# Expert weights loaded in pairs of pieces, the last expert's down product by column halves, and six unread products around the router

## The reference

```
def moe_swiglu(x, w_router, w_gate, w_up, w_down):
    logits = (x @ w_router).astype(jnp.float32)
    top_val, top_idx = lax.top_k(logits, TOP_K_EXPERTS)
    gate = jax.nn.softmax(top_val, axis=-1)
    ...
    for e in range(N_EXPERTS):
        out = out + combine[..., e:e + 1] * swiglu(x, w_gate[e], w_up[e], w_down[e])
    return out
...
    y = rms_norm(x, p['norm_final'])      # x * rsqrt(mean(x*x) + 1e-6) * gain
```

## Time and profile before

| | |
|---|---|
| median of 3 runs | 1419.91 us (1419.84 to 1422.66) |
| the profiled execution | 1420.81 us |
| its span, first to last instruction | 1419.0 us |
| PE busy | 1365.2 us, 96% of the span |
| DVE, ACT, POOL busy | 613.5, 235.9, 224.2 us |
| chain that ended last | PE 89%, DVE 8%, issue 1%, ACT 1% |
| the experts' stretch | from 718.66 us (first L1782) to 1403.4 us |
| expert weights | 384 loads of 704 KB, median 15.0 to 18.6 us from issue to landing |

### The profile page before, as it was taken

How to read it: one execution, slowest core, us unless ns; L and a number is a source line. 1 busy time by engine, 2 the same in 40 slices (tenths; PEclk the granted TensorE clock), 3 DMA queues, 4 the chain that set the end, 5 groups by cost and what they waited for, 6 DMA issues and landing times.

```text
span 1419.0 us, 39988 instructions
## 1 busy us (share of the span) xinstructions
PE 1365.2 (96%) x18034; PEld 981.8 (69%) x18034; DVE 613.5 (43%) x1252; ACT 235.9 (17%) x547; POOL 224.2 (16%) x271
## 2 busy tenths in 40 slices
PE   7899999999999999888899999999999999999996
PEld 5667899999997778777545656566565665656553
DVE  3599378677648467736232212120131202212153
ACT  3144121211016212413200000101000010000102
POOL 5147002121001433152030000000000000000100
PEclk9999999999999999989999999999999999999999
DMA  9554053433453300108969999999999999999992
GB/s 377 182 190 119 1 223 136 178 123 117 164 178 106 119 17 3 62 22 317 357 238 391 403 414 403 414 414 402 414 401 414 403 413 415 392 411 406 410 395 102
DMA packets 86020, 377.66 MB, mean 266 GB/s; under 512 B 11967, under 2 KB 12959, under 8 KB 85594
## 3 DMA queue, kind: packets, MB, share of 16 engines
q1 hardware_dynamic: 77712, 353.77, 63.8%
q0 software_dynamic: 4832, 17.17, 3.3%
q10 hardware_dynamic: 3306, 4.17, 0.8%
HBM read 367.15 MB, written 7.91 MB: 264 GB/s over the span
## 4 chain that ended last, share of the span: by engine, by line
PE 89%; DVE 8%; issue 1%; ACT 1%; DMA 0%; SPq 0%; DVEq 0%
PE bk L1782 32%; PE bk L1799 16%; PE bk L824 10%; PE bk L1081 10%; PE bk L1697 2%; PE bk L1029 2%; PE bk L1366 1%; DVE left L2409 1%; DVE tops L2407 1%; PE bk L1287 1%; PE bk L1248 1%; PE bk L1240 1%; PE bk L1232 1%; PE bk L1222 1%; PE bk L1214 1%
## 5 line engine op out<-in xcount | busy, mean ns | idle before, releaser
L1782 PE MATMUL bk<-part,xe 128*32 128x352 f32 x6144 | 458.9, 459 | 2.4 <-DVE xe L2972 2.4
L1782 PEld LDWEIGHTS bk<-part,xe 128*32 128x32 f32 x6144 | 252.7, 110 | 203.8 <-issue 105.5
L1799 PE MATMUL bk<-part,hidT 128*32 128x256 f32 x4224 | 232.6, 379 | 0.0
L1799 PEld LDWEIGHTS bk<-part,hidT 128*32 128x32 f32 x4224 | 151.6, 109 | 78.4 <-issue 1.0
L3040 DVE TENSOR_TENSOR hp<-sg,bk 128x352 f32<-128x352 f32 x48 | 37.3, 776 | 352.9 <-PE bk L1782 352.9
L824 PE MATMUL bk<-mx,ring 128*128 128x288 f32 x384 | 98.3, 415 | 0.0
L824 PE MATMUL bk<-xg,ring 128*128 128x288 f32 x336 | 87.5, 420 | 8.9 <-DMA ring<-in_weights 8.5
L824 PEld LDWEIGHTS bk<-mx,ring 128*128 128x128 f32 x384 | 73.4, 194 | 21.2 <-issue 0.8
L3066 DVE COPY ye<-bk 32x256 f32<-32x256 f32 x48 | 20.3, 422 | 150.8 <-PE bk L1799 150.1
L824 PEld LDWEIGHTS bk<-xg,ring 128*128 128x128 f32 x336 | 64.8, 196 | 27.8 <-issue 9.2
L3311 POOL TENSOR_TENSOR free_rows<-row_ss 128x1 f32 x7 | 5.4, 768 | 471.1 <-DVE xe L2981 447.1
(11 more groups left out here) (598 smaller groups left out, 1647.3 us busy)
## 6 DMA issues: line engine op xcount, KB each, us to landing
part<-in_moe_gate SPq DMA_DIRECT2D x128, 704.0 KB, 18.6
part<-in_moe_up SPq DMA_DIRECT2D x128, 704.0 KB, 18.0
part<-in_moe_down SPq DMA_DIRECT2D x128, 704.0 KB, 15.0
ring<-in_weights SPq DMA_DIRECT2D x121, 512.0 KB, 5.8
ro<-in_weights SPq DMA_DIRECT2D x8, 512.0 KB, 8.6
expert_rows<-ye ACTq DMA_DIRECT2D x7, 384.0 KB, 7.0
Ss<-in_states SPq DMA_DIRECT2D x1, 2048.0 KB, 7.9
out_wkv_sample<-Ss SPq DMA_DIRECT2D x8, 256.0 KB, 2.5
```

What stands on the lines that cost most here:

```text
L1782: last = mm(banks[g][32 * c:32 * c + 32, 0:FQ], xe[:, k, 32 * g:32 * g + 32], parts[PART_OF[ph]][:, FH * k + FQ * c:FH * k + FQ * c + FQ], ...
L1799: last = mm(down_bk[g // 2][32 * q:32 * q + 32, 256 * (g % 2):256 * (g % 2) + 256], hidT[:, half, g, 32 * m:32 * m + 32], parts[PART_OF[ph ...
```

## The change

Four things change.

1. **Layout and loads.** The gate, up and down weights of all experts are laid out ahead of the launch as one array `experts` [8 experts, 6 phases, 4 pairs, 128 partitions, 2816 numbers]. SP loads a pair of pieces with one transfer of 128 rows of 11264 bytes (`pair_load`), 192 transfers in place of 384, once PE has used both pieces of the pair 24 back.
2. **The last expert's down product** runs in column halves (`narrow_columns`): of each quarter of 256 columns, first the lower 128 of all 22 row blocks (into the down banks), then the upper 128 (into the gate banks). Between the last two passes PE scatters the lower half. `scatter`, `add_rows` and the end of the kernel take the columns as these interleaved halves; the squares of the lower half are summed, and `acc` times gain is formed (`acc_g`), while PE still works on the upper half.
3. **The end of the kernel** is by halves as well: ACT does the lower half (`first_columns`), DVE the upper one, the epsilon goes in with the root's bias, and the transfers wait for both. DVE's adding of the returned rows of experts 0 to 5 moves behind `hidden(0)` and `rows_turned` of the last expert.
4. **Six unread products** on PE: two behind L1717, two behind L1728 (512 and 256 columns), two behind the gather.

```
+def expert_pairs(inputs):
+    gate, up, down = (np.asarray(inputs[f"moe_{n}"])[0] for n in ("gate", "up", "down"))
+    wide = lambda w: w.reshape(NE, KC // 2, 2, P, 2, FH).transpose(4, 0, 1, 3, 2, 5)
+    low = down.reshape(NE, 2, P, KC // 2, 2 * FH).transpose(1, 0, 3, 2, 4)
+    packed = np.zeros((NE, 6, KC // 2, P, 2 * FH), np.float32)
...
-    SCATTER = ((0, 0), (0, 1), (1, 0), (1, 1), (2, 0), (2, 1))
+    SCATTER = ((0, 0), (1, 0), (2, 0), (0, 1), (1, 1), (2, 1))
-    DONE_AT = (2, 4, 6)
+    DONE_AT = (4, 5, 6)
+    columns = lambda x, half: x.rearrange("p (q h d) -> p h q d", q=4, h=2)[:, half]
+    def columns_out(copied, quarters, half):
+        banks = (bk[6:8], bk[0:2])[half]
+        for q in quarters:
+            for g in range(3):
+                last = copied(ye[32 * g:32 * g + 32, 256 * q + P * half:256 * q + P * half + P],
+                              banks[g // 2][32 * q:32 * q + 32, 256 * (g % 2):256 * (g % 2) + P])
+        return last
...
-        return (slot_in[i], _sum[i], 16) if part == 2 else (*pieces_in[KC // 2 * part + i // 2], 32)
+        return (slot_in[i // 2], _sum[i // 2], 16) if part == 2 else (*pieces_in[KC // 2 * part + i // 2], 16)
...
+        def pair_load(n):
+            e, ph, j = n // (6 * KC) % NE, n // KC % 6, n % KC // 2
+            sp.dma_start(parts[PART_OF[ph]][:, 2 * FH * j:2 * FH * (j + 1)],
+                         I["experts"][e, ph, j]).then_inc(piece_in(PART_OF[ph], 2 * j)[0], 16)
-            for n in range(6 * KC * NE):
+            for n in range(0, 6 * KC * NE, 2):
...
-                    done, first, per, value = piece_free(n - 3 * KC)
+                    done, first, per, value = piece_free(n + 1 - 3 * KC)
...
         last.then_inc(lg_mm, 1)
+        unread_product(7)
+        unread_product(6)
         pe.wait_ge(sel2_ok, 1)
...
         last.then_inc(rank_mm, 1)
+        unread_product(5)
+        unread_product(4, 256)
...
+        def narrow_columns(blk, ph, half, out_half):
+            banks = (down_bk, gate_bk)[out_half]
+            for m in range(NM):
...
+                for g in range(3):
...
+                    for q in range(4):
+                        at = D * m + 256 * q + P * out_half
+                        last = mm(banks[g // 2][32 * q:32 * q + 32, 256 * (g % 2):256 * (g % 2) + P],
+                                  hidT[:, half, g, 32 * m:32 * m + 32], parts[PART_OF[ph]][:, at:at + P],
...
+            narrow_columns(blk, 4, 0, 0)
...
+            narrow_columns(blk, 5, 1, 0).then_inc(down_mm, 1)
+            narrow_columns(blk, 4, 0, 1)
+            for g in range(3):
+                scatter(blk, g)
+            narrow_columns(blk, 5, 1, 1).then_inc(down_mm, 1)
...
         gather()
+        unread_product(7)
+        unread_product(6)
...
+        root_mean(0)
+        root_mean(1)
+        first_columns(0)
+        root_mean(2)
+        first_columns(1)
+        first_columns(2)
```

More of the change, by code:

```diff
@@ L185, in slots_of_weights @@
         packed[i, 0:t.shape[0], 0:t.shape[1]] = t
+    return packed
+def expert_pairs(inputs):
[3 more added lines that the diff above has]
+    packed = np.zeros((NE, 6, KC // 2, P, 2 * FH), np.float32)
+    for half in range(2):
+        packed[:, 2 * half] = wide(gate)[half].reshape(NE, KC // 2, P, 2 * FH)
+        packed[:, 2 * half + 1] = wide(up)[half].reshape(NE, KC // 2, P, 2 * FH)
+        packed[:, 4 + half] = low[half]
     return packed
@@ L448, in build @@
     got = sbt("got", [P, 2, D], at=starts["xT"])
+    acc_g = sbt("acc_g", [P, 3, 4, P], at=starts["xT"])
     token_no = sbt("token_no", [P, 3, 32])
@@ L1854, in _ @@
                 expert(blk, e)
-            for g in range(6):
+            for g in range(3, 6):
                 scatter(blk, g)
@@ L2259, in expert @@
                     nc.scalar.activation(sg2[:, g], gate_bk[g][:, 0:FQ], ACT.Silu).then_inc(silu_ok, 1)
+            if e == LAST:
+                act.wait_ge(rows_out, blk * (16 * LAST) + 16 * e)
+                for half in range(2):
+                    act.wait_ge(down_mm, blk * (2 * NE) + DOWN_N + 2 * e + 1 + half)
+                    columns_out(nc.scalar.copy, (0, 2), half).then_inc((ye_ok, scaled_mix_then_ye)[half], 1)
+                    if half == 0:
+                        for i, (t0, tn) in enumerate(TILES):
+                            act.wait_ge(sc_ok, blk * 6 + 6 + i + 1)
+                            unread = (xr[0:tn, 2, 0:512], xr[0:tn, 2, 512:D], bk[2][0:tn, :])[i].rearrange("p (q d) -> p q d", q=4)
+                            nc.scalar.activation(unread, columns(acc[0:tn, i], 0),
+                                                 ACT.Square, accum_out=pos[0:tn, i, 0:1])
+                return
             act.wait_ge(down_mm, blk * (2 * NE) + DOWN_N + 2 * e + 2)
@@ L3061, in expert @@
                 dve.wait_ge(rows_out, blk * (16 * LAST) + 16 * e)
+            if e == LAST:
+                dve.wait_ge(spot_then_rows, blk * 7 + 7)
+                for half in range(2):
+                    dve.wait_ge(down_mm, blk * (2 * NE) + DOWN_N + 2 * e + 1 + half)
+                    columns_out(V.tensor_copy, (1, 3), half).then_inc((ye_ok, scaled_mix_then_ye)[half], 1)
+                    for g in range(3 * half, 3 * half + 3):
+                        if g == 3:
+                            dve.wait_ge(sc_mm, blk * 6 + g + 1)
+                            V.tensor_scalar(ssf[:], pos[:, :, 0], 1.0 / D, EPS, ALU.mult, ALU.add)
+                        add_rows(blk, g)
+                    if half == 0:
+                        dve.wait_ge(sc_ok, blk * 6 + 6 + 3)
+                        for i, (t0, tn) in enumerate(TILES):
+                            V.tensor_tensor(acc_g[0:tn, i], columns(acc[0:tn, i], 0), columns(gain_f[0:tn], 0), ALU.mult)
+                return
             dve.wait_ge(down_mm, blk * (2 * NE) + DOWN_N + 2 * e + 2)
```

105 lines of the change are left out of this document (58 added, 47 removed).

## The result

| | kernel before | changed kernel |
|---|---|---|
| median of 8 runs | 1419.95 us (1418.27 to 1422.66) | 1424.19 us (1422.58 to 1425.62) |
| span of the profiled execution | 1419.0 us | 1423.7 us |
| its own time | 1420.81 us | 1425.62 us |

The ratio is 1.0026, 95% interval [1.0017, 1.0034]: the changed kernel is slower, by 4.2 us between the medians and 3.7 by the ratio. The range of the prediction (1416.8 to 1426.2) holds that; its middle, 1420.0, does not, and the time lies nearest to the rival with the chance of 0.07.

The account below looks back on a forecast made before the run. PE was taken to bound the kernel, DMA just behind. Scatter +2.0, tail -3.0 and router -0.65 gave -1.65, a transfer stall +1.65: span unchanged at 1419.0, time 1420.0 us, range 1416.8 to 1426.2.

Parts of the forecast that it names:

- the rival with the chance of 0.07: Last expert's down product: instructions don't arrive in time, 1056 products take up to 30.9 us, +2.6, 1422.6; chance 0.07.
- a stall of 1.65 us: Last expert's down1: PE waits for weights needed at 1386.1; 11.75 us less 10.1 saved by longer rows.
- longer rows save 10.1 us: Expert weight loads: 11264-byte rows take 7.0 ns less than two of 5632, over 1440 pairs of rows 10.1 us.
- The rival on the rows (0.3): Weight loads: longer rows save only 3.9 us, the stall in down1 is 7.9, end 1426.2; chance 0.3.
- Cost nothing, hidden by nothing: Last down product: 1056 records of 128 columns at 26.8 ns take 28.3 us, the same as the wide ones.
- The router: -0.65: Router: unread products keep PE's clock up, the gather ends 2.2 us earlier, of which 0.65 us is gained.
- The tail: -3.0: From the first copy to the end, working by halves: 12.6 us in place of 15.6, a gain of 3.0 us.
- C: Time of the first copy after the last expert's down product, 1403.43 us before; forecast to move by +2.0.
- nothing waits for them: DVE's later adds of returned rows: first needed some 8 us ahead of the first copy, so no cost.
- scatter ahead of C +2.0: PE's list: three lower-half scatter products before the first upper-half copy take 2.55 us, moving that copy by +2.0.

Follow-up runs that it names:

- experiment 3: Kernel before with the last expert's 256-column down products split into two of 128, old order, its down weights neither loaded nor waited for: ratio 1.0001.
- experiment 2: Kernel before with each 256-column product of the last expert's down product issued as two of 128, old order of passes: ratio 1.0052, 1427.6 us against 1419.2.
- column halves alone: Changed kernel with pieces of 5632 bytes instead of pairs and without the six unread router products: ratio 1.0071 to the kernel before, 1430.2 us.
- experiment 1: Kernel before with only the six unread router products added; pieces and last down product as before: ratio 1.0009 [0.9993, 1.0025].
- experiment 9: Changed kernel with two more unread router products, POOL's scaling held back, and one and a half unread products ahead of the final scatter: ratio 0.9994 to the kernel before.
- experiment 5: Kernel before with the expert weights loaded in pairs (11264-byte rows) and nothing else of the change: ratio 1.0045, 6.4 us slower.
- experiment 6: Kernel before with the pairs, and DVE's adds of returned rows moved behind the last expert's gates as in the change: ratio 0.9995.

## Why the prediction was right and wrong

That the time lies in the range is in part luck. The range reached up to 1426.2 for rows that save little, and their rate rose by what I said; what filled it was a cost of 4.5 us on the products that I had put at nothing, less a stall of 1.65 us that did not come. I forecast no change, and the kernel is slower by 0.17 to 0.34%.

- **Transfers: right in the rate and the landing, not in the stall.** I said that the last weights land near 1387.8 and that longer rows save 10.1 us (1.6% of a row's time); they land near 1387, and the rate rose by 1.7% over 540 us. The 1.65 us of stall did not come: by the chain above, PE would have wanted the last pair near 1387.8 even without its two waits for instructions (an estimate: product 192 of down1, which it reached near 1391.1, less 3.29 us), not at 1386.1. The estimate by "DMA: Bandwidth & Descriptors" of the Trainium skill, "Why small descriptors are slow" (0.84% saved), is too low for this case: 408 to 415 is 1.7%, and 414 to 423 in the stretch of rows 3 is 2.2%. The rival on the rows (0.3) fell with it. What of the gain is the rows' length is not shown: the pairs are also packed one behind the other in `experts`, where the pieces were cut out of wider rows, and no run separates the two.
- **The products: this step failed.** "Cost nothing, hidden by nothing" was worked out from 128 products in 3.70 us. That rate is right for one block of instructions, and the products themselves cost some 0.9 us in all (7.01, less 3.61 of waits and 2.53 of scatter). What I left out is that 528 wide products want a block every 7.0 us and 1056 narrow ones one every 3.7, while one comes every 6.2 us beside the weights. The wide product stood just inside that limit (in the trace of before its blocks start at 1381.01, 1387.96 and 1395.11); I looked at 128 products in rows 5, too few to use up a reserve. The rival with 0.07 had the mechanism, from the wait of 1.68 us behind 125 products; I argued it away with a reserve that is there, but lasts only 213 products. It had the price too low (2.6 us), as it took the rate of a stretch without weights. By "Runtime: NRT & Kernel Launch" of the Trainium skill, "Instruction fetch mechanics", fetching is hidden as dispatch is slower. That agrees with experiment 3 and not with experiment 2 (6.57 us of waits) or rows 10 (1.68 us): it is not hidden beside a queue of weights, nor behind products as dense as those of layer 1.
- **The router: -0.65 was wrong, there was nothing to gain.** I took DVE's read of the number of blocks as hidden behind the gather, between 0 and 1.1 us. Where the gather is long done, DVE's gap is 0.83 us (715.19 to 716.29, 1.10, in rows 6), so 0.27 was to be had. The earlier gather let POOL start early and hold DVE up by 0.85 us, more than that. I also missed the second clock loss: in the trace of before, 2.43 us idle ahead of the first expert product kept the clock; 3.20 us did not, and that cost 1.3. As two of the seven traces with the old router lose the clock there too, after 2.40 us idle (column halves alone, pairs alone), the worth of these products depends on which execution one compares with; by experiment 1 it lies between a gain of 1.0 us and a loss of 3.6.
- **The tail: -3.0 became -2.4,** and would be -3.75 with the clock kept (experiment 9). I had the scatter start 1.85 us behind C (it was 1.93, PE idle for 2.02) and did not ask what the clock does in that idle time. The clock costs 1.4. Against it, the end comes 3.0 us behind the last transfer's issue (1416.91 in experiment 9), where I had 3.7, so the two errors partly cancel.
- **The moved adds: "nothing waits for them" was right, and I did not see that they had to move.** With the pairs and the old place, the kernel is 6.4 us slower (experiment 5); with the adds moved, 0.9995 (experiment 6). I had costed the rows' length for the weights alone and never for the small transfers beside them.

The sum by terms, forecast and measured: router -0.65 and +1.86 (against a trace of before that was quick there); transfers +1.65 and 0; narrow products 0 and +4.5; scatter ahead of C +2.0 (2.55, less some 0.6 of waits and drains that I took to vanish) and +2.5; tail -3.0 and -2.4. That is 0 forecast and +6.5 measured, of which the earlier logits of that trace hide 1.8.

## What to carry to other kernels

Halving the width of matmuls doubles what the instruction queue must bring; count instructions per microsecond over a stretch much longer than the reserve, and look at what the DMA engines do then. A wait shortened ahead of one engine is worth what the next list allows, so read both ends of the gap before filling it, and ask what the idle time that is left does to the clock. A transfer made faster by longer rows can slow the short ones beside it, as it did here: look who waits for those.

## What the runs showed of the hardware

- A block of 256 instructions for PE came every 6.2 to 6.3 us beside a queue of weights with 5632-byte rows, at a DMA share of 1.0 and of 0.5 alike, and every 3.4 to 4.0 us without them (experiment 3, where that was as often as wanted; layer 1 of the kernel before, where PE waited all the same).
- Pairs with rows of 11264 bytes moved 415 GB/s from 780 to 1320 us, pieces with rows of 5632 bytes 408, at a DMA share of 1.01 and 1.02; the write of 384 KB by ACT beside them took 8.3 to 8.8 us by its median in the six traces with pairs, 6.9 to 7.2 in the eight without.
- The granted clock after idle time is not the same from one execution to the next: after 2.40 to 2.43 us idle ahead of the first expert product it was at 1.00 in five traces with the old router and at 0.50 in two (pairs alone, column halves alone).
- A small DVE copy (32x8) took 1.00 us in place of 0.15 when POOL's scaling of 128x1024 began beside it, in all four traces where the two met; the copies behind it took 0.15 again.
